# Down weights of the experts: from SyncE's DMA queue to ScalarE's own, issued after the expert's last copy

## What is computed

```python
def hierarchical_moe(x, w_group, b_group, w_router, b_router, w1, w3, w2):
    ...                                    # group by argmax, then the top 2 of its 8 experts
    def expert_block(args):
        xb, e = args
        return (jax.nn.silu(xb @ w1[e]) * (xb @ w3[e])) @ w2[e]
    ...                                    # weighted sum of both experts' rows for each token
```

## Time and profile before

| | |
|---|---|
| median of three runs | 2092.58 us |
| time of the profiled execution | 2092.59 us |
| its span, first to last instruction | 2090.8 us |
| expert stage, first gather to last result stored | 1033.9 to 2048.3 us |
| busy share of the span | PE 82%, DVE 26%, ACT 19%, POOL 19% |
| SP's queue q1 | 461.37 MB, 55.7% of the 16 DMA engines' span |
| POOL's queue q0, ACT's queue q10 | 27.02 MB and 22.04 MB |

### The profile page before, as it was taken

The page is one execution under the profiler, slowest core; times in us unless marked ns, Lnnn a source line. Parts: engine busy times, 40 slices in busy tenths (PEclk is TensorE's granted clock), DMA queues, the critical chain, the costliest instruction groups (busy, mean ns, idle before and its releaser), DMA issues.

```text
span 2090.8 us, 38753 instructions
## 1 busy us (share of the span) xinstructions
PE 1711.7 (82%) x13682; PEld 925.3 (44%) x13683; DVE 552.5 (26%) x1225; ACT 403.8 (19%) x915; POOL 402.4 (19%) x505
## 2 busy tenths in 40 slices
PE   7999999999999999999475577777777776766674
PEld 4676556644444444455343233444444433433342
DVE  6619223541122323266510011111111110110015
ACT  4011313311112111111111111221111211111113
POOL 1961002172151231001210011111111111110112
PEclk9999999999999999999698778998999988898788
DMA  7330411001111101562689999999999999999996
GB/s 218 136 63 6 151 40 46 21 21 40 50 40 50 41 31 34 186 269 96 272 354 427 426 413 410 412 397 398 411 409 400 408 408 413 417 410 413 420 366 255
DMA packets 96051, 511.10 MB, mean 244 GB/s; under 512 B 30256, under 2 KB 48688, under 8 KB 70896
## 3 DMA queue, kind: packets, MB, share of 16 engines
q1 hardware_dynamic: 79744, 461.37, 55.7%
q0 software_dynamic: 8816, 27.02, 3.5%
q10 hardware_dynamic: 7440, 22.04, 2.7%
HBM read 479.84 MB, written 34.35 MB: 246 GB/s over the span
## 4 chain that ended last, share of the span: by engine, by line
PE 51%; DMA 39%; DVE 4%; issue 4%; POOLq 1%; ACT 1%; SPq 1%; ACTq 0%; POOL 0%; DVEq 0%
DMA gain_b<-xf_rows,gather_idx 22%; DMA tokens<-expert_token_table 15%; PE act_bank L1069 14%; PE act_bank L839 13%; PE dve_bank L1069 6%; PE dve_bank L1135 5%; PE dve_bank L846 3%; PE act_bank L1235 2%; PE dve_bank L839 1%; PE act_bank L1247 1%; DMA unit<-in_w_in 1%; DVE unit L1575 1%; PE act_bank L846 1%; PE dve_bank L1052 1%; PE act_bank L1017 1%
## 5 line engine op out<-in xcount | busy, mean ns | idle before, releaser
L846 PE MATMUL dve_bank<-ident,gain_b 32*128 32x32 f32 x808 | 75.4, 238 | 247.1 <-DMA gain_b<-xf_rows,gather_idx 247.1
L1235 PE MATMUL act_bank<-unit,gain_a 128*32 128x256 f32 x3200 | 190.4, 391 | 24.9 <-issue 24.2
L2041 DVE TENSOR_TENSOR gain_a<-gain_a,act_bank 128x128 f32<-128x128 f32 x100 | 28.7, 287 | 680.4 <-ACT gain_a L1486 680.4
L1247 PE MATMUL act_bank<-unit,gain_a 128*32 128x256 f32 x2432 | 196.6, 479 | 8.9 <-DVE gain_a L2043 6.3
L846 PEld LDWEIGHTS dve_bank<-ident,gain_b 32*128 32x128 f32 x808 | 66.2, 155 | 292.3 <-issue 292.3
L1486 ACT ACTIVATE gain_a<-act_bank 128x128 f32<-128x128 f32 x101 | 28.0, 278 | 825.9 <-PE act_bank L1235 822.5
L1069 PE MATMUL act_bank<-norm_store,unit 128*128 128x512 f32 x384 | 168.7, 592 | 0.0
L788 POOL COPY gather_idx<-tokens 32x1 int32 x100 | 17.7, 177 | 768.5 <-DMA gain_b<-xf_rows,gather_idx 504.4
L1235 PEld LDWEIGHTS act_bank<-unit,gain_a 128*32 128x32 f32 x3200 | 104.9, 114 | 114.2 <-issue 55.6
L1069 PE MATMUL act_bank<-unit,unit 128*128 128x512 f32 x288 | 127.5, 592 | 0.0
L1247 PEld LDWEIGHTS act_bank<-unit,gain_a 128*32 128x32 f32 x2432 | 85.7, 132 | 77.4 <-issue 47.9
(11 more groups left out here) (307 smaller groups left out, 2028.4 us busy)
## 6 DMA issues: line engine op xcount, KB each, us to landing
unit<-in_w SPq DMA_DIRECT2D x112, 2048.0 KB, 37.9
norm_store<-in_w SPq DMA_DIRECT2D x32, 2048.0 KB, 34.4
mid_store<-in_w SPq DMA_DIRECT2D x32, 2048.0 KB, 34.6
rows_store<-in_w SPq DMA_DIRECT2D x16, 2048.0 KB, 46.4
unit_results<-side ACTq DMA_DIRECT2D x100, 128.0 KB, 6.3
unit<-in_w_gate SPq DMA_DIRECT2D x12, 1024.0 KB, 5.1
unit<-in_w_in SPq DMA_DIRECT2D x4, 2048.0 KB, 8.3
unit_results<-unit POOLq DMA_DIRECT2D x4, 2048.0 KB, 13.4
```

Source lines behind the costliest of these rows:

```text
L846: ins = nc.tensor.transpose(bank[:, n * rows:(n + 1) * rows], block_, ident[0:rows, 0:rows])
L1235: ins = nc.tensor.matmul(act_bank[0][h * CAP:(h + 1) * CAP, 0:2 * FQ].rearrange("t (w n) -> t w n", w=2), xT[:, k], w13[s][:, :, k, h * FQ ...
L1247: ins = nc.tensor.matmul(y_bank[s][z * CAP:(z + 1) * CAP, 0:DQ], hidT[:, j], w2s[s][:, j, z * DQ:(z + 1) * DQ], start=j == 0, stop=j == QU ...
L2041: v.tensor_tensor(hid, silu_g, act_bank[0][:, FQ:2 * FQ], ALU.mult).then_inc(per_slot["hid_ready"][s], 1)
```

## The change

The down weights of the fifth expert on are no longer started by SP. ACT starts them, on its own queue, after the last unit of the slot's expert: behind that unit's copies and its store of results. `each_unit` gets a `leave` hook that runs after a slot's last unit, and a range of turns, so that ACT walks turns 0 to 14 with the hook and turn 15 without it. SP's `refill` loses the wait for `y_ready` and the w2 transfer. The first four experts' weights are loaded as before.

```diff
-        def each_unit(eng, body, enter=None):
-
-            with eng.Fori(0, TURNS) as t:
+        def each_unit(eng, body, enter=None, turns=(0, TURNS), leave=None):
+
+            with eng.Fori(*turns) as t:
...
                     with eng.Fori(first, end) as c:
                         body(c, s, in_sequence(c, shift), t, own)
+                    if leave:
+                        leave(s, t)
...
             def refill(e, s):
                 first = sp.value_load(spans[0:1, 0, bass.ds(e, 1)], min_val=0, max_val=SLOT_UNITS)
                 chosen_expert = sp.value_load(spans[0:1, 4, bass.ds(e, 1)], min_val=0, max_val=E - 1)
-                up, down = expert(bass.ds(chosen_expert, 1))
+                up = expert(bass.ds(chosen_expert, 1))[0]
...
                 expert_up(up, s)
-                sp.wait_ge(per_slot["y_ready"][s], first)
-                expert_down(down, s)
...
+            def refill_down(s, t):
+                chosen_expert = act.value_load(spans[0:1, 4, bass.ds(t * SLOTS + (SLOTS + s), 1)], min_val=0, max_val=E - 1)
+                act.dma_start(w2s[s].rearrange("p k n -> p (k n)"),
+                              w2[0][bass.ds(chosen_expert, 1)].rearrange("e (p k) n -> p (e k n)", p=P)
+                              ).then_inc(down_loaded[s], 16)
+
             gate(1)
-            each_unit(act, unit_work, result_rows)
+            each_unit(act, unit_work, result_rows, (0, TURNS - 1), refill_down)
+            each_unit(act, unit_work, result_rows, (TURNS - 1, TURNS))
```

## The result

| | before | after |
|---|---|---|
| median of four runs | 2092.4 us | 2142.8 us |
| range | 2090.1 to 2093.6 | 2139.7 to 2145.9 |
| ratio of the times, 95% interval | 1 | 1.024 (1.0227 to 1.0252) |
| profiled execution | 2092.59 us | 2140.66 us |
| last result stored (start of the store) | 2046.4 us | 2093.7 us |

The change makes the kernel 50 us slower. The forecast was slower by 24.4 us: the direction is right, the size is half of what came.

The account below looks back on a forecast made before the run. The prediction took bytes through full DMA engines to bound the expert stage, with the gather chain just beneath. Later tables and up weights, 8.4 us, plus idle engines, 16, made 24.4 on 2092.6: 2117 us, range 2088.4 to 2145.

Parts of the forecast that it names:

- SP loses a wait: SP's 62.1 us wait for down matmuls goes, but its wait for hidden rows always ends later: worth 0.
- ACT gains work: ACT's 60 register loads and DMA issues, 1.0 to 1.3 us per expert, hide in its waits for up matmuls: 0.
- w2 comes later: The w2 issue on ACT comes 7 to 15 us later, but is needed 27 us later at the least: worth 0.
- The order of bytes: In its own queue w2 runs ahead, so tables and up weights land later in the expert stage: +8.4 us.
- Gathers slower by 0.83 us: Each gather meets w2 packets as a third stream on the DMA engines: 0.83 us more, bounds 0 and 2.9 on average.
- What that does to the slack: In the stretch of many units the late gather chain outruns the queued backlog and DMA engines idle: +16 us.
- Stores behind w2: Result stores on ACT's queue lie behind a w2, holding ACT, then PE; named under one rival, no term in the sum.
- long turns: Rival: DMA engines take long turns per queue, gathers rise 2.9 us on average; +38 to +96 us, 2160; chance 0.11.
- watch list: Signs expected in the profile after; the forecast fails if ACT waits over some 10 us in total for its stores.
- Order only: Rival: gathers are no slower and only w2 running ahead costs; +4.2 to +15 us, 2101; chance 0.18.
- Nothing seen: Rival: gains and losses cancel as all bytes still pass through full engines; 2088.4 to 2096.8 us; chance 0.10.
- faster: Rival: two queues keep the DMA engines better fed, 22 us off and 8.4 back for order, 2079; chance 0.11.

Follow-up runs that it names:

- e1: The kernel after, with each store reading rows nothing writes and ACT's wait for the slot's last store gone (wrong results): 2122.88 us, ratio 1.0153.
- e5: The kernel before, with one memset of an unused row block on POOL ahead of each gather: 2098.23 us, ratio 1.0021.
- e9: The kernel before, with two memsets of unused row blocks on POOL ahead of each gather: 2129.06 us, ratio 1.0179.
- e3: The kernel after, with every expert cut to one unit, the first 32 of its tokens: 2068.13 us.
- e4: The kernel before, with every expert cut to one unit, the first 32 of its tokens: 2061.35 us.
- e10: The kernel after, with each w2 issued one expert later, stores reading unused rows and no wait for the last store (wrong results): 2122.53 us, ratio 1.0142.
- e7: The kernel after, with each w2 in two transfers of 1 MB, rows of 8 KB, on ACT's queue: 2207.24 us, ratio 1.0545.
- e6: The kernel after, with each w2 issued one expert later by ACT: 2140.25 us, ratio 1.0221.

## Why the prediction was right or wrong

**The account.** Over 1100:2000 all kernels have the same bytes to move. What is not moved by 2000 us, at the 411 GB/s of the kernel before, is transfer time missing. It belongs to the execution that was profiled, so it is compared with that execution's time. The kernel before moved 370.25 MB; the table gives what the others moved. The rows, of the kernel before, e1, e5 and e9:

```profile
1100.00:2000.00 900.00, 629.09 (x9336) 348.35 (x9332) 99.06 (x270) 157.68 (x450) 98.68 (x178) 0.88 1.01 411
```

```profile
1100.00:2000.00 900.00, 637.32 (x9164) 347.44 (x9152) 97.58 (x266) 154.43 (x443) 97.48 (x176) 0.87 0.99 401
```

```profile
1100.00:2000.00 900.00, 633.21 (x9276) 349.61 (x9280) 98.72 (x267) 156.01 (x445) 183.38 (x268) 0.87 1.00 407
```

```profile
1100.00:2000.00 900.00, 631.53 (x8998) 343.31 (x9001) 95.60 (x259) 150.37 (x430) 261.27 (x347) 0.86 0.97 395
```

| kernel | MB | transfer missing, us | profiled execution above 2092.6 us | left over, us | median above before, us |
|---|---|---|---|---|---|
| e5: gathers slower, one queue | 366.46 | 9 | 8.5 | -1 | 5.9 |
| e9: the same, stronger | 355.89 | 35 | 33.6 | -1 | 35.9 |
| e1: after, no wait for stores | 360.84 | 23 | 24.8 | 2 | 28.9 |
| after | 351.25 | 46 | 48.1 | 2 | 50.4 |

The missing transfer accounts for each of the four to 2 us. The stores are worth about 20 us (after against e1: 19.9 by the medians, 18 by the ratios, 23 by the profiled executions). The other 29 are the slower gathers and the order of bytes together. How they divide isn't measured: e3 and e4 give 6.8 for the order where gathers don't bind, but in the full stage only some 2 us are left over for a loss outside the missing transfer, and e10 gained nothing. There the order acts at least in part through the same empty engines, since it makes the gather chain late before the stretch begins.

**SP loses a wait, worth 0: right.** The wait of 62.1 us is gone, and that for the hidden rows, 409.5 us in the earlier trace rows, is now 819.7. No gain shows.

**ACT gains work, worth 0: right as far as it is seen.** An issue took 0.39 us against the 0.33 assumed, and ACT still has 767.7 us of waits for up matmuls to hide it in. The change of loops falls between the last w2 (2040.93) and the next silu (2044.28), where ACT waits for PE. Only where a store has made ACT late does its own work show: 15.9 us in 4 waits, 3.2 in 1 in e1. That lies within the stores' 20.

**w2 comes later, worth 0: right** for the change: PE has no wait for w2 in the list of its waits. "Some 15 us" from issue to landing was right too: by the packet records the last row of a w2 is through 15.7 us after its start in the median (7.4 to 23.4), and its rows are 10.2 us on the way. e7 shows where that ends, when q10's share falls to a third.

**The order of bytes, +8.4: right by e3 and e4, its size in the full stage open.** e3 less e4 is 6.8. In the full stage the first gather of the stretch, 1262.24 in the earlier trace rows, starts at 1270.87, 8.6 us later. Slower gathers alone don't do this: it is 1.8 us later in e5 and 0.5 earlier in e9.

**Gathers slower by 0.83 us: right.** The landing in 1262:1700 of the kernel after, where the earlier trace rows has 7.2:

```profile
DMA to landing us min/median/max: 2.9/8.0/9.4
```

The cycle is (1681.74 - 1270.87)/42 = 9.78 us; 9.7 was forecast, and in e1, without the waits for stores, it is 9.48. The turns of one row on which this value rested are there (section 5). Some luck is in it: the five gathers of the earlier trace rows moved 0.42 MB, 102 rows of 4 KB and not 160, and the engines were at times idle beside the gathers measured here (the quickest landed in 2.9 us). The Trainium skill ("DMA: Bandwidth & Descriptors", section "Queues, rings and completion order") has the engines go round the queues by packets, and the runs agree: 569 packets against 566. It has a packet hold some 9 to 17 descriptors; the turn measured here is one row of 16 KB (the other queue 16 places on in 86% of the cases), and the measurement decides.

**What that does to the slack, +16: the sum near, its reasoning not.** e1, which has gathers and order alone, stands at 28.9 (24.8 in the profiled execution) where the forecast had 24.4. Slack was read straight from the tables' landing times, which contain 6 to 7 us that a small transfer takes anyway (section 3); 8.6, 11.5 and 18.0 were really some 2, 5 and 12. And the engines ran dry earlier than I let them: already 1260:1350 has 0.93 after and 0.94 in e1, before the table of 1401. Against that the chain fell behind less than reckoned: e1's 62nd gather is 37 us late and not 43. Gathers that land faster beside idle engines, as I had reckoned, may be the cause; no run separates it. So the two errors, less slack and less delay, set each other off in part, and that is luck.

**Stores behind w2: the step that failed.** The sum has no term for them. I saw the queue, and gave the delay as part of the rival "long turns" only, as if a store were held up by a long turn. It isn't: turns were short, and the store still waits until the w2 ahead of it on its own queue have gone, at half the rate, some 10 us for each 2 MB (2.1 MB at half of 409 GB/s). The margin was misread too. The slot's next copies come 8.85 us after the first of its last copies, but the store starts 1.8 us behind that. In the kernel before (the first line's wait is one of the two that make 1.4 us):

```profile
1303.55 1.58 ACT L1495 ACTIVATE side<-act_bank 32x256 f32<-32x256 f32 x4 [0.46 <-DMA unit_results<-side]
1305.37 0.32 ACTq L1499 DMA_DIRECT2D unit_results<-side  x1
```

8.85 less 1.8 less 6.4 leaves 0.6 us of room, and not the 2.4 that the two numbers of the prediction suggest, against up to 10 of w2. This could have been priced from the trace of the kernel before. It cost about 20 of the 26 us by which the forecast fell short; the other 4 to 6 are the gathers and the order. In the watch list, "ACT waits for its own stores by more than some 10 us in total" was the condition under which the forecast fails; it was 88.9.

**The shares and the end.** For 1350:1600 I expected 15 to 20 us short; 250 x (1.01 - 0.94) is 17. What I didn't expect is 90 x (1.01 - 0.93) = 7 us ahead of it and 400 x (1.01 - 0.97) = 16 us behind, in a stretch where in e1 the engines are full (1.01, 409 GB/s): this part is the stores'. The last store moved to 2093.7 and not to about 2070.

**The rivals.** "Order only" is out by the gathers' 8.0. "Long turns" gives a better time (2160), and the measured 50 us lie in its +38 to +96, for a wrong reason: 9 us or more per gather did not come, and turns are one row. "Nothing seen" and "faster" are out; the rate at full share stays at 417 GB/s with two queues and with one. The Trainium skill ("DMA: Bandwidth & Descriptors", section "Rules for kernel authors") says that spreading over queues doesn't help bandwidth; e3 and e4 agree with 417 and 417. That it does no harm either does not follow: the total rate was untouched, and the kernel lost 2.4%.

**Open.** How the 29 us of e1 divide between slower gathers and the order of bytes, and why a later w2 (e6, e10) loses in the middle what it gains at the start of the stretch, no run here shows.

## What to carry to other kernels

A queue is an order. Before bulk loads are moved to another queue, list the small transfers that already use it, take for each the time until somebody waits for it, and subtract the drain time of the bulk load at its share of the rate; here 0.6 us of room stood against up to 10. Where a chain of small dependent transfers paces a stage just under the byte bound, price each added microsecond of their latency times the length of the chain less the real slack, and take the latency of an ordinary small transfer off a landing time before you call it slack.

## What the runs showed of the hardware

- With two queues full, the 16 DMA engines serve them one row each in turn: 191 and 192 weight rows of 16 KB in 15 us, alternating in 86% of the cases, and 423 of 16 KB and 424 of 8 KB in 25 us. Bytes are shared as the row sizes are: 3.13 to 3.28 MB with equal ones, 6.94 to 3.71 with one queue's halved.
- A gather of up to 32 rows of 4 KB lands in 2.9 us beside idle engines, 7.2 (median) beside one bulk queue and 8.0 (median) beside two.
- A store of 128 KB lands 6.4 us after its start beside another queue's bulk load. With w2 ahead of it on its own queue it took 13.1 and 18.0 us in the cases read, and its first row started 0.9 us after the last row of w2 in the first of them.
- The rate of full engines is the same with one bulk queue and with two, 417 GB/s in e3 and e4. In the full stage, with more gathers in the mix, the kernel before has 404 to 412.
